# Conditioning columns and rounded attention outputs in one gated stage, the opening's weights ahead of the rows, and transposes between the first projection's groups

## The reference

```python
mod_x = silu(c) @ w_ada[l] + b_ada[l]            # six columns of 1024: sh1, sc1, g1, sh2, sc2, g2
h_x = modulate(x, sh1, sc1)                      # layer_norm(x) * (1 + scale) + shift
p_x = h_x @ w_in[l]                              # keys, values, queries and the gates' logits
y_f = fourier_mix(f_in) @ w_fo
y_m = attend(q_m, k_m, v_m) @ w_mo
y_g = attend(q_g, k_g, v_g) @ w_go
g_f, g_m, g_g = split(sigmoid(gate_logits + b_gate))
mix = (g_f * y_f + g_m * y_m + g_g * y_g) @ w_o
x = layer_norm(alpha * x + g1 * mix, ln1_g, ln1_b)
x = layer_norm(alpha * x + g2 * sq_relu_mlp(modulate(x, sh2, sc2)), ln2_g, ln2_b)
```

## Time and profile before

| what | before |
|---|---|
| runs | 3415.57, 3420.51, 3423.50 us |
| the profiled execution | 3413.63 us, span 3411.6 us, 2.0 us outside it |
| TensorE | 3144.0 us busy, 92% of the span |
| VectorE, ScalarE, GpSimd | 58%, 29%, 28% |
| mean granted clock of TensorE | 0.961 of full speed |
| opening and layer 0's projection | 0 to 206 us |
| gated stage of layer 0, of layer 1 | 526 to 865 us, 1889 to 2109 us |

### The profile page before, as it was taken

How to read it: one execution, slowest core, us unless ns; L and a number is a source line. 1 busy time by engine, 2 the same in 40 slices (tenths; PEclk the granted TensorE clock), 3 DMA queues, 4 the chain that set the end, 5 groups by cost and what they waited for, 6 DMA issues and landing times.

```text
span 3411.6 us, 37992 instructions
## 1 busy us (share of the span) xinstructions
PE 3144.0 (92%) x15196; PEld 2461.1 (72%) x15196; DVE 1984.4 (58%) x3016; ACT 1002.8 (29%) x1749; POOL 942.7 (28%) x708
## 2 busy tenths in 40 slices
PE   6998999999999999989899999899988989989798
PEld 3985666777578888879575665588878856777576
DVE  4576774444665555583677354666665855667344
ACT  3135771000231111141366100322222135431352
POOL 1004766331210000010177654200000325531262
PEclk9999999999999999989899999999999988999799
DMA  6411004343222121123101555132212310023100
GB/s 204 156 53 28 10 29 130 105 108 106 80 75 74 50 74 61 63 80 120 28 1 38 165 162 188 50 115 99 99 51 92 108 50 1 32 80 102 50 1 25
DMA packets 206335, 268.26 MB, mean 79 GB/s; under 512 B 29280, under 2 KB 133680, under 8 KB 205648
## 3 DMA queue, kind: packets, MB, share of 16 engines
q1 hardware_dynamic: 204080, 265.83, 24.2%
q10 hardware_dynamic: 2080, 0.01, 0.0%
HBM read 255.17 MB, written 10.52 MB: 78 GB/s over the span
## 4 chain that ended last, share of the span: by engine, by line
PE 39%; DVE 6%; ACT 2%; POOL 2%; issue 2%; DMA 1%; SPq 0%; DVEq 0%; ACTq 0%; POOLq 0%
PE ps L367 14%; PE ps L1911 5%; PE ps L1921 4%; PE ps L2401 2%; PE ps L1323 2%; PE ps L1306 1%; PE ps L1694 1%; PE ps L2731 1%; PE ps L1276 1%; PE ps L2676 1%; PE ps L1088 1%; PE ps L3085 1%; DVE U L2846 0%; DVE U L1433 0%; PE ps L2690 0%
## 5 line engine op out<-in xcount | busy, mean ns | idle before, releaser
L746 POOL TENSOR_TENSOR ht_lo<-HT,ht_hi 128x1024 fp32r<-128x1024 f32 x28 | 69.3, 2474 | 1071.6 <-DVE X L704 627.0
L1911 PE MATMUL ps<-ht_hi,w_hi 128*128 128x512 f32 (+1 forms) x832 | 286.6, 344 | 18.2 <-POOL ht_lo L746 9.8
L1911 PE MATMUL ps<-ht_lo,w_hi 128*128 128x512 f32 (+1 forms) x832 | 285.2, 343 | 0.0
L1911 PE MATMUL ps<-ht_hi,w_lo 128*128 128x512 f32 (+1 forms) x832 | 285.0, 343 | 0.0
L1921 PE MATMUL ps<-w_hi,a_hi 128*128 128x512 f32 x640 | 251.8, 393 | 4.3 <-DVE a_lo L2036 4.3
L1921 PE MATMUL ps<-w_hi,a_lo 128*128 128x512 f32 x640 | 250.5, 391 | 0.0
L1921 PE MATMUL ps<-w_lo,a_hi 128*128 128x512 f32 x640 | 250.4, 391 | 0.0
L367 PE MATMUL ps<-w_lo,ht_hi 128*128 128x320 f32 (+2 forms) x800 | 244.2, 305 | 0.0
L1490 POOL TENSOR_TENSOR p_lo<-ring,p_hi 128x512 fp32r<-128x512 f32 x156 | 199.9, 1291 | 113.3 <-DVE p_hi L1445 87.5
L367 PE MATMUL ps<-gate_ht_hi,gate_w_hi 128*128 128x512 f32 (+1 forms) x576 | 224.1, 389 | 1.5 <-POOL w_lo L397 1.5
L367 PE MATMUL ps<-U,ring 128*128 128x512 f32 (+1 forms) x576 | 217.9, 521 | 0.0
(11 more groups left out here) (415 smaller groups left out, 8005.0 us busy)
## 6 DMA issues: line engine op xcount, KB each, us to landing
ring<-w_dram SPq DMA_DIRECT2D x30, 2048.0 KB, 8.0
U<-w_ada_dram SPq DMA_DIRECT2D x80, 512.0 KB, 3.7
ring<-w_in_dram SPq DMA_DIRECT2D x48, 512.0 KB, 5.9
ring<-w_in_dram SPq DMA_DIRECT2D x8, 1280.0 KB, 5.8
ring<-a_w_in_dram SPq DMA_DIRECT2D x8, 1280.0 KB, 6.8
ring<-w_ada_dram SPq DMA_DIRECT2D x4, 2048.0 KB, 10.9
hi_scratch<-ht_hi SPq DMA_DIRECT2D x2, 3072.0 KB, 10.0
gate_ht_hi<-hi_scratch SPq DMA_DIRECT2D x8, 768.0 KB, 4.5
```

The source lines that it names most:

```text
L746: pool.tensor_tensor(HT_LO[:, :, tokens], HT[:, :, tokens], HT_HI[:, :, tokens].bitcast(F32), ALU.subtract).then_inc(ht_ready.sem, 1)
L1911: last = pe.matmul(ps[:, g % 4, 0:c1 - c0], lhsT, rhs, start=(k + j == 0), stop=(k == KD - 1 and j == 2))
```

## The change: what it does

1. **Opening.** The two `w_ada` loads are issued ahead of x; the context rows are loaded by ScalarE's queue after the first evacuation. ScalarE, not VectorE, evacuates the four products, with the six square roots between them: after evacuations 0 and 1 two roots each, after 2 and 3 one each. The transposes of `MODROW` now wait for the biases' addition (`bias_taken`).
2. **First projection.** Only two tiles are transposed ahead of it; tile g+2 is transposed ahead of group g.
3. **Conditioning columns.** `early` is gone. Layer 0's gated stage carries twelve units in its eight slots: `of` gives slots 2 to 5 two units each. In those the quarters stand after the evacuations of groups 0, 1 (first unit) and 3, 5 (second), the first unit's sums ahead of group 3 and the second's ahead of the next slot's group 1.
4. **Rounded attention outputs.** `OT` is split into `OT_HI` (ScalarE, in the place of X) and `OT_LO` (VectorE), and `w_mo`, `w_go` are split too: 8 pieces per slot on GpSimd instead of 6. The y of branches 1 and 2 is 12 rounded matmuls instead of 4 fp32 products. ScalarE rounds the first two slots' weights; it starts after its last work of attention.
5. **X** is reloaded late, after the last use of `OT_HI`, in two or three transfers; the last slot takes branch 0 last. One sigmoid buffer per half of the tokens instead of three.

The core of the diff:

```diff
@@ start
+                    first_loads(sp, lambda s: None)
                     sp.dma_start(X[:, 0:XT, :], A["x"]...).then_inc(x_loaded.sem, 16)
-                    first_loads(sp, lambda s: None)
-                    sp.dma_start(X[:, XT:NT, :], A["ctx"]...).then_inc(ctx_loaded.sem, 16)
@@ ada_first
-                @b.vector
-                def _(dve):
+                @b.scalar
+                def _(act):
+                    roots = [(0, 1), (2, 3), (4,), (5,)]
                     for c in range(n):
-                        dve.tensor_copy(MODROW[:, c * 512:(c + 1) * 512], ps[0:2, 5 + c % 2, :])...
+                        act.activation(MODROW[:, c * 512:(c + 1) * 512], ps[0:2, 5 + c % 2, :], ACT.Copy)...
+                        if c == 0:
+                            act.dma_start(X[:, XT:NT, :], A["ctx"]...).then_inc(ctx_loaded.sem, 16)
+                        for t in roots[c]:
+                            root(act, p, t, t)
@@ class Macs
+            def of(self, slot):
+                if len(self.units) == KD:
+                    return [slot]
+                return [slot] if slot < 2 else [2 * slot - 2, 2 * slot - 1] if slot < 6 else [slot + 4]
+            def sums_at(self, slot, g, G):
+                if g == (2 if G == 3 else 1) and slot:
+                    return self.of(slot - 1)[-1]
+                return self.of(slot)[0] if g == 3 and len(self.of(slot)) > 1 else None
+            def beside(self, dve, slot, g):
+                units = self.of(slot)
+                last = self.of(slot - 1)[-1] if slot else -1
+                if len(units) == 1:
+                    if g == 1:
+                        self.take(dve, last)
+                        self.pieces(dve, units[0], 0, 2)
+                    if g == 2:
+                        self.pieces(dve, units[0], 2, 4)
+                elif g in (0, 3):
+                    self.take(dve, units[0] if g else last)
+                    self.pieces(dve, units[g // 3], 0, 2)
+                elif g in (1, 5):
+                    self.pieces(dve, units[g // 5], 2, 4)
@@ gemm, the load queue
-                            if macs:
-                                macs.sp(sp, i * 2 + s)
+                            for u in macs.of(i * 2 + s) if macs else ():
+                                macs.sp(sp, u)
                             sp.wait_ge(mm_done.sem, i * (2 * G) + mm_done.n + (s + 1) * G)
@@ gated
+                if br == 0:
+                    out = [(w[:, 24 + k, :], FT[:, k, c[0]:c[1]]) for k in range(4)]
+                else:
+                    out = [p for k in range(4) for p in parts(*y_weights(s, br, k),
+                                                              OT_HI[:, (br - 1) * 4 + k, c[0]:c[1]],
+                                                              OT_LO[:, (br - 1) * 4 + k, c[0]:c[1]])]
...
+                    weights(0, slice(0, 4))
+                    act.wait_ge(pv_done.sem, pv_done.n)
+                    for j in range(KD):
+                        act.wait_ge(o_taken.sem, o_taken.n - H2 + 2 * j + 2)
+                        act.activation(OT_HI[:, j, 0:nq * P], OT[:, j, 0:nq * P], ACT.Copy)...
+                        if j == 3:
+                            weights(0, slice(4, PIECES))
...
+                        for q, (br, what) in enumerate(pieces_of(u)):
+                            if u > 1:
+                                for cols, hi in parts_of(s, br, what):
+                                    last = pool.tensor_tensor(hi, ring[s][:, cols], one[:, 0:hi.shape[1]], ALU.mult)
...
+                    sp.wait_ge(mm_done.sem, mm_done.n + N * G - len(halves))
+                    x_again(sp, l)
@@ the layers
+                if l == 0 and g + 2 < NT:
+                    turn_tile(pe, now, g + 2, XNS[:, g + 2, :], 2 * (g % 2))
                 pe.wait_ge(ht_ready.sem, now.ht + g + 1)
-            early = Macs([(1, part, half) for part in (0, 1) for half in range(2)], 2, 0) if l == 0 else None
-            macs = Macs([(l, part, half) for part in (2, 3, 4, 5) for half in range(2)], 1 if last else 2, 7)
+            units = [(l, part, half) for part in (2, 3, 4, 5) for half in range(2)]
+            if not last:
+                units += [(l + 1, part, half) for part in (0, 1) for half in range(2)]
+            macs = Macs(units, 1 if last else 2, 7)
```

More of the change, by code:

```diff
@@ L313, in first_loads, with gemm @@
                         d.then_inc(ring_full[s].sem, 16)
-        def gemm(G, mms, evac, depth, split=None, join=True, ready=None, loads=None, macs=None, behind=None, between=None):
+        def gemm(G, mms, evac, depth, split=None, join=True, ready=None, loads=None, macs=None, behind=None, between=None, pieced=None):
             n, parts, issue = streams[at_stream[0]]
@@ L767, in _ @@
                                           ALU.subtract, ALU.mult).then_inc(xn_ready.sem, 1)
-                @b.scalar
-                def _(act):
-                    for t in range(NT):
-                        root(act, p, t, t)
-            ada_first()
+            ada_first(p)
             with block(False) as b:
@@ L781, in _ @@
                 def _(pe):
-                    for t in range(NT):
+                    for t in range(2):
                         turn_tile(pe, p, t, XNS[:, t, :], 2 * (t % 2))
@@ L1577, in mms, with pieced @@
                                                              GATE_HT[:, k, c[0]:c[1]], HT_LO[:, k, c[0]:c[1]])]
-                return [(2 * br, n, gates),
-                        (2 * br + 1, n, [(w[:, 24 + br * 4 + k, :], ins[br](k, c)) for k in range(4)])]
+                if br == 0:
[4 more added lines that the diff above has]
+                                                              OT_LO[:, (br - 1) * 4 + k, c[0]:c[1]])]
+                return [(2 * d, n, gates), (2 * d + 1, n, out)]
+            def pieced(pe, u, g, m, k):
+                br, c = order(u)[g]
+                if c != halves[0]:
+                    return
+                what = k // 12 if m == 0 and k in (0, 12) else "y" if m and br and k == 0 else None
+                if what is not None:
+                    s = u % 2
+                    pe.wait_ge(w_split[s].sem, w_split[s].n + u // 2 * PIECES + pieces_of(u).index((br, what)) + 1)
             def evac(b, n):
@@ L1591, in _, with weights @@
-                    loop(n, body)
+                    def weights(u, which):
+                        act.wait_ge(ring_full[u].sem, ring_full[u].n + 16 * 6)
+                        for br, what in pieces_of(u)[which]:
+                            for cols, hi in parts_of(u, br, what):
+                                last = act.activation(hi, ring[u][:, cols], ACT.Copy)
+                            last.then_inc(w_rounded[u].sem, 1)
+                    weights(0, slice(0, 4))
+                    act.wait_ge(pv_done.sem, pv_done.n)
@@ L1634, in loads @@
                 w1_chunk(sp, l, 1, 0)
-                macs.sp(sp, KD)
+                macs.sp(sp, len(macs.units))
             nc.sync.wait_ge(pv_done.sem, pv_done.n)
@@ L1727, in _ @@
                         residual(1, 0)
-                        macs.take(dve, KD - 1)
+                        macs.take(dve, len(macs.units) - 1)
                         norms(0, residual(0, 1))
```

200 lines of the change are left out of this document (124 added, 76 removed).

## The result

The changed kernel took 3446.29 us, median of 4 runs (3443.70 to 3455.24); the kernel before 3419.11 us, median of 4. The ratio is 1.0084, 95% interval 1.0070 to 1.0099. Run again later beside other kernels it was 1.0072 (1.0053 to 1.0090). It is slower by some 29 us (24 to 34). The profiled execution took 3445.23 us, 31.6 us above the profiled execution of before, 3413.63.

What follows compares the result with a forecast made beforehand. TensorE, busy 92% of the span, was taken as the bound. Terms of -42.9 and +55.3 gave +12.4 us on the profiled 3413.63, 3426; on the median 3432 us was forecast, own range 3422 to 3445, full range 3388 to 3455.

Steps and rivals of the forecast that it cites:

- The fp32 products: Both gated stages: replacing fp32 products with rounded matmuls saves 17.3 us in layer 0 and 11.5 us in layer 1.
- The waits: Layer 0's gated stage: TensorE waits for multiply-adds slowed by GpSimd, 39 us in sum, bounds 2.4 and 50 us.
- The clock: After five waits above 6 us, half clock costs 2 us more each: +10 us (0 to 12).
- The opening: Before the first projection: weights land some 5 us earlier, transposes start near 48.3 us; -0.7 us, bounds -4 and +4.
- Between the groups: First projection, tiles transposed between groups: the load's end moves from 86.70 to about 82 us, -4 us (0 to -7).
- The projection: Layer 0's projection: the 7.53 us wait and its half-clock stretch go, -9.4 us together.
- The handovers: Attention to gated stages: first gate product 2.1 us later in layer 0, 2.5 in layer 1; +6.3 us with clock (4 to 9).
- What costs nothing: Splitting OT, X's late reload (issued 13 us before the stage ends) and layer 1's GpSimd pieces were claimed to cost nothing.
- layer 1's GpSimd as the bound: Rival in layer 1's gated stage: eight pieces exceed the slot, six slots lose 2 us and more; +32 us, 3453, chance 0.1.
- the quarters in time: Rival in layer 0's gated stage: waits only 2.4 us, no clock falls; -34 us, 3386, chance 0.13.
- half in time: Rival in layer 0's gated stage: partial overlap, about 20 us of waits, no clock; -17 us, 3404, chance 0.2.
- The opening's rival: Rival in the opening: VectorE's norms end last, +4 instead of -4.7 us, within the range; no separate chance.

Runs made afterwards that it cites:

- poolwait: Changed kernel, but in layer 0's two-unit slots GpSimd waits for the first unit's four quarters before splitting the next weights; 3436.46 us, 1.0049.
- acthi0_wait: Changed kernel with GpSimd held back until the first unit's quarters are done, and ScalarE rounding the gated weights in layer 0 only; 3411.97 us, 0.9982.
- opening: Changed kernel with the new opening undone (x ahead of the first weights, VectorE evacuates), transposes between the projection's groups kept; 3439.51 us, 1.0067.
- turns: Changed kernel with all six tiles transposed ahead of the projection's first group again; 3445.93 us, 1.0083.
- wofirst: Changed kernel, but in layer 1 X's later rows are loaded behind the second half of w_o; 3440.09 us, 1.0070.
- best12: acthi0_wait with the edits of wofirst and opening, all twelve units in layer 0's gated stage; 3401.07 us, 0.9951 against before.
- after2: The changed kernel run again, unaltered, beside other kernels; 3442.30 us, 1.0072 against before.

## Why the prediction was right, and where its sizes were off

The direction, the place and the mechanism were right: slower, by four slots in layer 0's gated stage where TensorE waits for multiply-adds at 1.57 us. The sum was too small, +12.4 us forecast on the profiled execution and +31.6 measured. The median, 3446.29 us, lies just above the forecast's own range (3422 to 3445); only the range of all cases holds it, and that reaches so far for the sake of a rival that did not come. That part is luck. Step by step:

- **The fp32 products, right.** Forecast 0.72 and 0.36 us a group, measured 0.74 and 0.28: 8 x 2 x 1.02 = 16.3 us in layer 0. Layer 1 gave 9.9 us of the 11.5.
- **The waits, right.** Forecast 1.6, 10, 7, 7, 7 and 6.4 us, 39 in all; measured 0.7 (ahead of slot 2), 7.9, 7.2, 6.7, 7.8 and 5.6, 35.9. Slot 2 was over-sized by 2 us. That contention with GpSimd, not position, sets them is shown by `poolwait` (0.31 us each) and `acthi0_wait`. The page "SBUF — State Buffer" of the Trainium skill ("SBUF: two separate sides") has the one that comes second wait for the other's whole length. The trace agrees with it in direction and not in size: in strict turns the eight would have taken about 15 us by the forecast's estimate, and they took 12.57.
- **The clock, mis-sized: this is the first term that failed.** I took +2 us for each wait over 6 us, from the 3.87 us stretch of the earlier trace rows; measured 17.5 us for five, 3.5 each. The slow stretch behind a wait of 7 us was 7 to 10 us long three times of five. In `poolwait` a wait of 4.55 us already had it, where I had put the edge above 6, and in `acthi0_wait` one of 0.89 us. The one row I took it from was near the short end. That waits of 2 to 3 us leave the clock alone in the trace of before was a wrong reading besides: in its opening, behind a wait of 2.27 us (to 54.33) and around three more of 1.9 to 2.8 us, the granted clock is 0.50 for 12 us:

```profile
56.00:68.00 12.00, 5.92 (x26) 5.21 (x27) 7.42 (x7) 11.90 (x29) 8.44 (x4) 0.50 0.16 7
```

- **The opening, wrong, and mostly by the clock again.** Forecast -0.7 us; it costs some 2.5. The first product did start at 10.55 and the third at 30.50, as worked out, but the second of these by luck: I had taken 8.65 us from issue to landing out of a row that names VectorE, not the load, as what ended the wait. Now the load was issued at 20.08, a microsecond earlier than forecast, and the product started 10.42 us later. Then the third and fourth products ran in part at half clock (16.63 us for their 32 matmuls, against 13.89):

```profile
10.55 16.36 PE L374 MATMUL ps<-ring,stat 128*2 128x512 f32 x32 [5.79 <-issue]
30.50 16.63 PE L374 MATMUL ps<-ring,stat 128*2 128x512 f32 x32 [3.58 <-DMA ring<-w_ada_dram]
50.76 1.83 PE L515 MATMUL ps<-ident,U 2*128 2x2 f32 x16 [3.63 <-DVE modc L488]
52.52 3.68 PE L754 MATMUL ps<-ident,U 128*128 128x128 f32 x16
```

  So the fourth ended at 47.1 us, where I had 44. What follows it, its evacuation, the last tile's root behind that on ScalarE, that tile and the biases on VectorE, took 3.63 us where I had 4.3, and the transposes start at 50.76, where I had 48.3. They and the first tiles' (last two rows) were slow as well: `opening` has 1.14 and 1.97 us for them.

- **Between the groups, right by itself.** Forecast -4 us at the end of the load, measured -4.9 (91.21 in `turns`, 86.33 in after), but beside the new opening only 0.4 us of it was left (86.33 against 86.70 in the earlier trace rows).
- **The projection, right.** The 7.53 us wait is gone; the longest left is 1.43 us. Opening, turns and projection together were forecast at -14.1 and came to -15.2 + 5.1 = -10.1, the 5.1 being the three sums that stood inside the stretch before.
- **The handovers, right.** TensorE's wait for the first rest rose by 2.2 us (forecast 2.1) and by 2.7 (forecast 2.5), the latter against the earlier trace rows:

```profile
514.59 0.77 PE L374 MATMUL ps<-gate_ht_hi,gate_w_hi 128*128 128x512 f32 x1 [2.98 <-POOL w_lo L1705]
...
1926.52 0.47 PE L374 MATMUL ps<-gate_ht_hi,gate_w_hi 128*128 128x512 f32 x1 [3.40 <-POOL w_lo L1705]
```

- **"What costs nothing" was wrong for the late reload of X.** I had its issue 13 us ahead of the stage's end, which holds in layer 0. In layer 1 SyncE's queue has it behind the loads of the bias row, which wait for a store, and it is issued 1.8 us ahead of the end:

```profile
2133.35 0.33 SPq L581 DMA_DIRECT2D mod_scratch<-U  x1
2137.32 0.53 SPq L600 DMA_DIRECT2D U<-b_ada_dram  x2
2137.90 0.35 SPq L1587 DMA_DIRECT2D X<-x_scratch  x1
...
2139.24 0.71 SPq L1748 DMA_DIRECT2D U<-w_o_dram  x1
```

  The 2 MB then go ahead of `w_o`'s second half, and TensorE waits for that, after:

```profile
2152.88 8.51 PE L1815 MATMUL ps<-U 128*128 128x512 f32 x16 [6.08 <-DMA U<-w_o_dram]
```

  before:

```profile
2121.59 7.11 PE L1694 MATMUL ps<-U 128*128 128x512 f32 x16 [2.72 <-DMA U<-w_o_dram]
```

  The stage grew by 5.7 us. `wofirst` takes back 3.6: most of the loss is shown to be that order, the rest is not settled.

The terms that failed are then the clock (+7.5 us beyond the forecast), the opening (+3), X in layer 1 (+5.7), and 1.6 us less gained in layer 1's products. With 3 us less of waits that is +15 of the 19 us between forecast and measurement; the rest, some 4 us, lies in stages that differ by as much between executions of unchanged code, and stays open.

Of the rivals, layer 1's GpSimd as the bound did not come (213.2 us, no wait of the kind); the quarters in time or half in time did not either. The opening's rival came in part: of its -4.7 us, 0.4 were there at the end of the first load.

## What to carry to other kernels

Elementwise work that is "free" beside TensorE has two prices that its own duration hides: what it takes when another engine gets in its way (here twice as long, beside GpSimd), and the half clock behind the waits that it causes (here half as much again as the waits). Before two such jobs are put in one slot, lay out both engines' stretches in time, and look for an engine that does not slow the other: here GpSimd was held back and ScalarE took half of its work, and the change's loss of 0.8% became a gain of 0.2% (`acthi0_wait`), and of 0.5% with the old opening and the order of the loads mended as well (`best12`). A load that is moved late has to be followed through its queue, behind what else waits there, in every layer separately.

## What the runs showed of the hardware

ScalarE rounds a 128x512 piece every 0.52 us (four in 2.18), half of GpSimd's 1.04, and it did not slow VectorE. In `acthi0_wait` it rounded from 618.19 on, four pieces in the first row and the others by 622.55, and the eight multiply-adds that began at 619.66 took 6.32 us, as long as alone:

```profile
618.19 2.18 ACT L1674 ACTIVATE gate_w_hi<-ring 128x512 fp32r<-128x512 f32 x4
...
619.66 6.32 DVE L630 SCALAR_TENSOR_TENSOR U<-U,stat 128x512 f32<-128x512 f32 x8
```

Between VectorE and GpSimd the slowing goes both ways. In `poolwait` GpSimd's roundings took 1.04 us and its rests 1.28 while VectorE was idle, and 1.49 and 1.62 us once its multiply-adds had begun at 632.63.

The length of the half-clock stretch is not constant for code that is the same: in layer 0's attention, behind idle times of 1.5 and 1.4 us, after's clock was low for more than 8 us (two windows of it),

```profile
442.00:446.00 4.00, 4.00 (x12) 2.33 (x10) 2.18 (x4) 0.73 (x2) 0.50 (x1) 0.50 0.00 0
446.00:450.00 4.00, 4.00 (x15) 3.01 (x14) 1.39 (x4) 2.29 (x5) 2.51 (x2) 0.50 0.00 0
```

and in `wofirst`, with the same code up to there, behind one of 1.5 us for under 4:

```profile
430.00:434.00 4.00, 4.00 (x13) 3.18 (x12) 2.04 (x5) 2.99 (x7) 0.75 (x1) 0.57 0.45 122
434.00:438.00 4.00, 4.00 (x19) 2.47 (x18) 3.82 (x8) 2.46 (x5) 2.39 (x2) 1.00 0.18 75
```

From that wait to the same instruction two steps on it is 34.1 us in after (430.31 to 464.44) and 29.5 in `wofirst` (429.60 to 459.13), 4.6 us of difference for the same code (`after2` had the long stretch again), and in one profile of each kernel it looks like an effect.
